# An encoder with two expert layers: the overflow blocks reordered, and identity products placed in the routing

## The reference, cut to what matters

```python
def expert_block(args):
    xb, e = args
    return (jax.nn.silu(xb @ w_gate[e]) * (xb @ w_up[e])) @ w_down[e]
yb = lax.map(expert_block, (xs, block_expert)).reshape(cap, D)
out = out.at[slot_tok].add(yb.astype(jnp.float32) * slot_w[:, None])
```

## Time and profile before

| what | value |
|---|---|
| median of 3 runs | 1425.97 us (1424.84 to 1427.04) |
| profiled execution, its own time | 1427.76 us |
| its span | 1426.0 us |
| TensorE busy | 1287.0 us (90%) |
| VectorE busy | 969.6 us (68%) |
| ScalarE busy | 618.0 us (43%) |
| share of the chain that ended last | PE 77%, DVE 12%, ACT 4%, DMA 4% |
| mean DMA rate | 251 GB/s over the span |

### The profile page before, as it was taken

The page is one execution under the profiler, slowest core; times in us unless marked ns, Lnnn a source line. Parts: engine busy times, 40 slices in busy tenths (PEclk is TensorE's granted clock), DMA queues, the critical chain, the costliest instruction groups (busy, mean ns, idle before and its releaser), DMA issues.

```text
span 1426.0 us, 14722 instructions
## 1 busy us (share of the span) xinstructions
PE 1287.0 (90%) x5057; PEld 864.6 (61%) x5057; DVE 969.6 (68%) x1379; ACT 618.0 (43%) x795; POOL 160.6 (11%) x169
## 2 busy tenths in 40 slices
PE   2999899949999999987999999998499999999886
PEld 2566665536666667743788854467367666667432
DVE  8678875576777777726766587856667777776153
ACT  3486401235555555504222167734355555554002
POOL 6000000010000000011000057710100000000200
PEclk9999899969999999999899999999599999999999
DMA  9636674258999999894365230024589999998641
GB/s 352 227 111 244 221 278 164 94 200 300 370 365 366 368 377 376 308 362 150 103 252 177 89 118 1 1 74 159 220 317 372 376 369 364 372 376 304 232 188 59
DMA packets 78114, 347.81 MB, mean 244 GB/s; under 512 B 12500, under 2 KB 12684, under 8 KB 69104
## 3 DMA queue, kind: packets, MB, share of 16 engines
q1 hardware_dynamic: 67184, 325.70, 61.4%
q0 software_dynamic: 7344, 16.68, 3.3%
q10 hardware_dynamic: 3536, 4.79, 0.9%
HBM read 334.15 MB, written 23.07 MB: 251 GB/s over the span
## 4 chain that ended last, share of the span: by engine, by line
PE 77%; DVE 12%; ACT 4%; DMA 4%; issue 2%; POOL 0%; SPq 0%; DVEq 0%; ACTq 0%; POOLq 0%
PE ps L1911 24%; PE ps L1922 16%; PE ps L2023 9%; PE ps L1831 4%; PE ps L1902 3%; PE ps L1793 3%; PE ps L1838 2%; PE ps L1897 2%; PE ps L1798 2%; DVE scratch L1027 2%; PE ps L2067 2%; PE ps L2095 2%; PE ps L2081 2%; DMA x_res<-in_x_dram 1%; DVE slab_ring_r L1449 1%
## 5 line engine op out<-in xcount | busy, mean ns | idle before, releaser
L1922 PE MATMUL ps<-slab_ring,scratch 128*128 128x512 f32 x560 | 246.5, 593 | 3.4 <-ACT scratch L935 2.1
L1911 PE MATMUL ps<-slab_ring_r,gate_rows_r 128*128 128x512 f32 x512 | 202.1, 395 | 0.0
L1922 PEld LDWEIGHTS ps<-slab_ring,scratch 128*128 128x128 f32 x560 | 105.8, 190 | 124.2 <-issue 117.2
L1449 DVE TENSOR_TENSOR slab_ring_r<-slab_ring,h_t_r 128x2048 fp32r<-128x2048 f32 x64 | 143.9, 2288 | 16.8 <-ACT h_t_r L852 16.8
L2023 PE MATMUL ps<-slab_ring_r 128*128 128x512 f32 x384 | 123.1, 402 | 4.1 <-DVE h_t_r L1084 4.1
L852 ACT ACTIVATE h_t_r<-slab_ring 128x2048 fp32r<-128x2048 f32 x64 | 118.6, 1901 | 0.0
L1911 PE MATMUL ps<-h_t_r,gate_rows_r 128*128 128x512 f32 x256 | 105.7, 413 | 12.5 <-issue 7.6
L881 ACT ACTIVATE scratch<-ps,mod_ab 128x128 f32<-128x128 f32 x128 | 48.1, 456 | 143.8 <-PE ps L1897 143.8
L1911 PEld LDWEIGHTS ps<-slab_ring_r,gate_rows_r 128*128 128x128 f32 x512 | 97.9, 191 | 19.2 <-issue 0.5
L1911 PE MATMUL ps<-h_t_r,scratch_r 128*128 128x512 f32 x256 | 102.9, 402 | 0.0
L1449 DVE TENSOR_TENSOR slab_ring_r<-slab_ring,mod_ring_r 128x2048 fp32r<-128x2048 f32 x32 | 73.3, 2292 | 41.0 <-ACT mod_ring_r L852 41.0
(11 more groups left out here) (343 smaller groups left out, 2303.0 us busy)
## 6 DMA issues: line engine op xcount, KB each, us to landing
slab_ring<-in_expert_w_gate_dram SPq DMA_DIRECT2D x35, 2048.0 KB, 9.5
slab_ring<-in_expert_w_up_dram SPq DMA_DIRECT2D x35, 2048.0 KB, 9.9
slab_ring<-in_expert_w_down_dram SPq DMA_DIRECT2D x35, 2048.0 KB, 9.7
mod_ring<-in_mod_w_dram SPq DMA_DIRECT2D x40, 512.0 KB, 4.5
y_rows<-scratch SPq DMA_DIRECT2D x32, 512.0 KB, 10.3
slab_ring<-in_mod_w_dram SPq DMA_DIRECT2D x32, 512.0 KB, 4.8
slab_ring<-in_mod_w_dram SPq DMA_DIRECT2D x12, 1024.0 KB, 11.5
slab_ring<-in_w_qkv_dram SPq DMA_DIRECT2D x6, 2048.0 KB, 12.0
```

The costliest lines, as they stand in the source:

```text
L1449: tt_(rest, w, top.bitcast(F32), ALU.subtract).then_inc(low_ready[c], 1)
L1911: ins = pe.matmul(ps[:, bank, :], x, w, start=(kt == 0 and i == 0), stop=(kt == KT - 1 and i == 2))
L1922: ins = pe.matmul(ps[:, 5 + h, :], hidT[:, f, :], w[:, 2 * f + h, :], start=(f == 0), stop=(f == FT - 1))
```

## The change

It has these parts.

- **Turning inside the last step.** The rows of overflow block 0 are turned inside the last expert's step, before its up product, and scaled there by ScalarE and VectorE (`xst_over(0)`). Rows of block k+1 are turned after the down product of block k, ahead of its mixing. The wait for `yb_ready` now stands behind the gate and up products. TensorE reads `n_over` in step 1.
- **Sums moved on VectorE.** `over_mask` is parted from the scaling, `combine(0)` now stands ahead of `over_hid(0)`.
- **Table load moved.** ScalarE ends `experts` with a root of a spare column, so that the table for Sqrt is loaded there.
- **SP.** The store of the last expert's output in layer 0 is issued before the load of the second `w_qkv` slab, not before the third.
- **POOL.** The gather of overflow block 0 is unconditional.
- **Loops.** On TensorE each turn of the overflow loop has three Ifs in place of one, on ScalarE two.
- **Identity products.** `keep_clock(n)` puts n fp32 products of the 128x128 identity with itself into PSUM bank 3: 6 ahead of the last `turn_x`, 3 ahead of the last `logits`, 26 ahead of the rank sums, 17 ahead of the second slot sum and 14 ahead of step 0, in each layer. Nothing reads them.

```diff
 SP, layer 0
                 for w, used in enumerate((gate_done, up_done, down_done)):
+                    if w == 1:
+                        store(NE - 1, 1)
                     sp.wait_ge(used, e0 + NE)
-                    if w == 2:
-                        store(NE - 1, 1)
                     load_slab(("qkv", w), w_qkv[:, :, w * HALF:(w + 1) * HALF])
...
 ScalarE
+            act.wait_ge(up_done, e0 + NE - 1)
+            xst_over(0)
             take_hid(NE - 1)
...
                 with act.If(k < n_over):
-                    act.wait_ge(o["turned"], k + 1)
-                    for kt in range(4):
...
+                with act.If(k + 1 < n_over):
+                    xst_over(k + 1)
+            act.activation(spare[:, l:l + 1], eps[:, 0:1], ACT.Sqrt)
...
 VectorE
+                if last:
+                    v.wait_ge(up_done, e + e0)
+                    xst_over(0)
                 v.wait_ge(silu_done, e + (e0 + 1))
...
             with v.If(n_over > 0):
-                over_in(0)
+                over_mask(0)
+            combine(0)
+            with v.If(n_over > 0):
                 over_hid(0)
-            for t in range(TT):
+            for t in range(1, TT):
                 combine(t)
...
                     with v.If(k < n_over):
+                        xst_over(k)
                         over_y(k)
                         for t in range(TT):
                             over_add(k, t)
-                        over_in(k)
+                        over_mask(k)
                         over_hid(k)
...
 TensorE
+            def keep_clock(products):
+                for _ in range(products):
+                    pe.matmul(ps[:, 3, 0:P], ident[:, :], ident[:, :], start=True, stop=True)
...
+            keep_clock(6)
             turn_x(s, TT - 1)
+            keep_clock(3)
             logits(TT - 1)
+            keep_clock(26)
             pe.wait_ge(hot_ready, TT * (l + 1))
...
             ins.then_inc(slots_summed, 1)
+            keep_clock(17)
...
+                if last:
+                    pe.wait_ge(o["xs"], 16)
+                    turn_xs(0, o["turned"])
                 pe.wait_ge(low_ready[1], 2 * e + (2 * e0 + 2))
...
             turn_xs(0, xs_turned)
+            keep_clock(14)
             step(0, 0, 0, first=1)
...
-            pe.wait_ge(yb_ready, e0 + NE)
...
                 with pe.If(k < n_over):
-                    pe.wait_ge(o["xs"], (k + 1) * 16)
-                    pe.wait_ge(o["added"], k * TT + 1)
-                    turn_xs(0, o["turned"])
+                    pe.wait_ge(o["added"], k * TT + 2)
                     pe.wait_ge(o["xst"], (k + 1) * 2)
...
                     product(over_slab[1], 3, o["gu"])
+                    pe.wait_ge(yb_ready, e0 + NE)
...
                     down(over_slab[2], o["down"])
+                with pe.If(k + 1 < n_over):
+                    pe.wait_ge(o["xs"], k * 16 + 32)
+                    turn_xs(0, o["turned"])
+                    pe.wait_ge(o["xst"], k * 2 + 4)
+                    pe.sem_inc(turn_seen, 1)
+                with pe.If(k < n_over):
                     pe.wait_ge(o["yb"], k + 1)
```

More of the change, by code:

```diff
@@ L192, in build @@
     eps = small("eps", [P, 1])
+    spare = small("spare", [P, LAYERS])
     modc = small("mod_cols", [P, KT])
@@ L697, in gather_over @@
                                       bounds_check=S - 1, oob_is_err=False).then_inc(o["xs"], 16)
-            with gp.If(n_over > 0):
-                gather_over(0)
+            gather_over(0)
             for par in range(2):
@@ L916, in experts, with xst_over @@
                     step(2 * i + par, par, i)
+            o = over[l]
+            def xst_over(k):
+                act.wait_ge(o["turned"], k + 1)
+                for kt in range(4):
+                    ins = act.activation(xsT[0][:, kt, :], ps[:, 0, kt * P:(kt + 1) * P], ACT.Identity, bias=AB[:, s, 1, kt:kt + 1], scale=AB[:, s, 0, kt:kt + 1])
+                ins.then_inc(o["xst"], 1)
             step(NE - 2, 0, NE // 2 - 1)
             step(NE - 1, 1, NE // 2 - 1, last=True)
+            act.wait_ge(up_done, e0 + NE - 1)
+            xst_over(0)
             take_hid(NE - 1)
-            o = over[l]
-            act.wait_ge(route_ready, l + 1)
             n_over = act.value_load(info[0:1, 7:8], min_val=0, max_val=MAX_OVER)
@@ L925, in experts @@
                 with act.If(k < n_over):
-                    act.wait_ge(o["turned"], k + 1)
-                    for kt in range(4):
-                        ins = act.activation(xsT[0][:, kt, :], ps[:, 0, kt * P:(kt + 1) * P], ACT.Identity, bias=AB[:, s, 1, kt:kt + 1], scale=AB[:, s, 0, kt:kt + 1])
-                    ins.then_inc(o["xst"], 1)
                     act.wait_ge(o["gate"], k + 1)
@@ L1520, in experts, with xst_over @@
                 step(2 * i + 1, 1, i)
+            o = over[l]
+            def xst_over(k):
+                v.wait_ge(o["turned"], k + 1)
+                for kt in range(4, KT):
+                    ins = ts(xsT[0][:, kt, :], ps[:, 1, (kt - 4) * P:(kt - 3) * P], AB[:, s, 0, kt:kt + 1], AB[:, s, 1, kt:kt + 1], ALU.mult, ALU.add)
+                ins.then_inc(o["xst"], 1)
             step(NE - 2, 0, NE // 2 - 2)
+            v.sem_inc(o["added"], TT)
             step(NE - 1, 1, NE // 2 - 1, last=True)
             take_y(NE - 1, 1, NE // 2 - 1)
-            o = over[l]
             n_over = v.value_load(info[0:1, 7:8], min_val=0, max_val=MAX_OVER)
@@ L1533, in experts, with over_mask @@
             link(tt_(early_w, early_w, both_w, ALU.mult))
[L1534 to L1541, removed]
+            def over_mask(k):
                 ts(match, yplace[:, 0, :], block_no, None, ALU.is_equal).then_inc(o["mask"], 1)
@@ L1940, in step @@
                 pe.wait_ge(xst_dve, e + (e0 + 1))
+                if first == 2:
+                    pe.wait_ge(route_ready, l + 1)
+                    n_over = pe.value_load(info[0:1, 7:8], min_val=0, max_val=MAX_OVER)
                 if first != 1:
@@ L1956, in step @@
                     turn_xs(1 - par, xs_turned)
+                if last:
+                    pe.wait_ge(o["xs"], 16)
+                    turn_xs(0, o["turned"])
                 pe.wait_ge(low_ready[1], 2 * e + (2 * e0 + 2))
                 split_product(par, 1, 3, range(KT)).then_inc(up_done, 1)
+                if first == 2:
+                    return n_over
+            o = over[l]
             pe.wait_ge(xs_filled[0], (NE // 2) * l * 16 + 16)
             turn_xs(0, xs_turned)
+            keep_clock(14)
             step(0, 0, 0, first=1)
-            step(1, 1, 0, first=2)
+            n_over = step(1, 1, 0, first=2)
             with pe.Fori(1, NE // 2 - 1) as i:
@@ L1970, in experts @@
             down_product(NE - 1, 1, NE // 2 - 1)
-            o = over[l]
             over_slab = [slab(("exp", l, c, 0)) for c in range(3)]
-            pe.wait_ge(yb_ready, e0 + NE)
-            pe.wait_ge(route_ready, l + 1)
-            n_over = pe.value_load(info[0:1, 7:8], min_val=0, max_val=MAX_OVER)
             pe.sem_inc(o["mixed"], TT)
```

## The result

The changed kernel takes 1412.76 us (median of 4 runs, 1411.52 to 1414.12) against 1425.9 for the kernel before beside it: ratio 0.9902, 95% interval 0.989 to 0.9915. The forecast was 1401.0 (1393 to 1409). The sign was right, but only about half of the 25 us came. The profiled execution took 1413.72 us, its span is 1412.0 (before 1427.76 and 1426.0).

A forecast was written before the change was run, and what follows sets the result against it. The kernel was taken as TensorE-bound (77% of the chain), with gains only where TensorE waits or its clock falls. 3.3 + 1.7 + 10.3 + 9.7 = 25.0 us off the median 1425.97 gave 1401.0, range 1393 to 1409.

The forecast's parts named there:

- Part 1: Routing: identity products keep TensorE's clock up, half gates fall to 2.77 us; 3.3 us in layer 0, 1.7 in layer 1.
- clock not held: Rival in the routing: identity products don't hold the clock and cost 0.45 us each; 1417 us, chance 0.06.
- loads not overlapped: Rival in the routing: weight loads don't pass beside products at full clock, a product takes 0.43 us; 1414, chance 0.04.
- slower: Rival in the routing: loads don't overlap and the clock is lower, 0.87 us a product; 1477 us, chance 0.02.
- Part 2: Layer 0's overflow: rows turned in step 15, products follow at once, scaling starts 9.0 us earlier; 10.3 us (2 to 12.5).
- Each lands after 5.4 to 5.7: Layer 0's overflow: the first two y gathers land by 639.3, so hidden rows start at 642.1, 0.7 us late.
- second `w_qkv` slab: Layer 0's overflow: loaded 11 us later but wanted only some 40 us later, so it costs nothing.
- The 8.4 us from mixing to turn: Layer 0's overflow: six empty loop turns on TensorE's sequencer, 1.4 us each, put the next turn 8.4 after mixing begins.
- Part 3: Layer 1's overflow: first block gains, second block's gate product starts earlier, table load saves 1.2; 9.7 us (7 to 13).
- The first block gains as in layer 0: Layer 1's overflow: products end at 1351.4 instead of 1358.8, the down product 7.1 us earlier at 1361.2.
- forecast wait of 1.9 us for the second block's rows: Layer 1's overflow: these rows land at about 1363, after the down product ends at 1361.2, so TensorE waits 1.9 us.
- the hidden rows wait for the gathers: Rival in the overflow: gathers take 7.7 and 9.5 us, layer 0 keeps 2, layer 1 about 5; 1414, chance 0.08.

The follow-up runs named there:

- e4: The kernel before with the 6, 3, 26, 17 and 14 identity products alone: 1422.5 us, ratio 0.9968.
- e9: The changed kernel with the two w_qkv slabs held until the last y rows have landed, in layer 0 only: 1407.5 us, ratio 0.9864.
- e2: The changed kernel with w_qkv slabs (layer 0) and the second overflow block's weights (layer 1) held until the last y rows landed: 1397.9 us, ratio 0.9807.
- e5: e2 with TensorE's second overflow-loop branch nested inside the first, so an empty turn has one branch instead of three: 1397.9 us, ratio 0.9802.
- e1: The changed kernel with the first overflow block's hidden rows ahead of combine(0) on VectorE, as before the change: 1418.9 us, ratio 0.9949.
- e3: The changed kernel with both edits, loads held as in e2 and hidden rows ahead of combine(0) as in e1: 1403.1 us, ratio 0.9833.
- e6: e5 with the second block's rows gathered ahead of the y rows, turned behind the first block's up product and scaled behind the hidden rows: 1397.5 us.
- e10: The changed kernel with only the second overflow block's weights in layer 1 held until the last y rows have landed: 1403.5 us, ratio 0.9836.
- e11: e6 with, in layer 1, the first block's output scaled ahead of VectorE's last pair of adds: 1398.0 us, ratio 0.9792.
- e8: e2 with ten more identity products ahead of step 1's gate product in each layer, into an idle PSUM bank: 1397.5 us, ratio 0.9795.

## Why the prediction was right or wrong

**Part 1 was right.** An identity product costs 0.23 us at 2.4 GHz (0.22 taken). The products hid, but for the last 14 (4.92 against 3.1 us), and the half gates went to 2.78 us in layer 0 and 3.01 in layer 1 by the chain. I had expected one fall of the clock ahead of the 17 and full clock behind; they ran at full clock (34 records in 4.04 us), and the fall came within the 14. Layer 0 gave 2.15 + 0.8 = 3.0 of 3.3 us, layer 1 1.8 of 1.7; e4 confirms it alone. The rivals "clock not held", "loads not overlapped" and "slower" are out. The rule of the Trainium skill ("TensorE: Matmul & The Clock Gate", The mechanism) that a weight load overlaps a running matmul only when the row group differs would have made a product 0.43 (the prediction's estimate, twice its 0.22); the trace, with 0.23, doesn't agree.

**Part 2 failed in one step**: "Each lands after 5.4 to 5.7". I took that landing from a stretch in which one slab had been under way for 8 us, and put two whole slabs behind the store without asking what they do to the gathers behind it. They landed after 11.5 to 12.0 us. The same oversight stands in the term of the second `w_qkv` slab, "loaded 11 us later": I put it at nothing, because I looked only at who wants the slab and not at what it meets. e9, which holds the slabs back, gives 5.3 us. No run tests SP's old order alone. The store itself was timed well (3.2 against 2.6). From this follow the hidden rows forecast 0.7 late (TensorE waited 4.86 us for them) and, what counted, the other six adds forecast to end at 650.7: they waited for gathers three times more (1.56 us the longest) and ended at 654.63. From the last down product's start to the scaling it was 40.93 us before; I forecast 31.1, the changed kernel has 36.74 and e2 30.53. So 3.4 of the 9.0 came, and all of it with the loads held. The rest of layer 0 was mis-sized the other way: from the scaling on I counted 1.3 and measured 3.6 (332.23 to 328.67); 2.8 of them lie in the QKV stage, of which less ran at the lower clock (from its first product to attention's first 148.91 us before, 146.12 after). I had no term for this, so this part of the gain is luck. The 8.4 us from mixing to turn were right: 8.55, and e5 shows why.

**Part 3 failed in the same way, and worse.** "The first block gains as in layer 0" overlooked that the earlier gate product calls up the next block's weights among the gathers. Of 9.7 us 3.95 - 0.8 = 3.1 came. With that load held it was 12.8. The forecast wait of 1.9 us for the second block's rows did not appear, because all else was later; e1 shows what they cost once it is not.

**The rival** "the hidden rows wait for the gathers", given 0.08 and 1414, hit the time and the place. Its price in layer 0 (2 us kept) was off by 5, in layer 1 (5 kept) by 2, and e1 shows that in layer 0 the hidden rows' wait is a symptom: the adds that wait for the last gather bind. My argument against it, that the slab is behind the store now, was the mistake: behind the store is in front of the gathers. With the loads held both layers together gave 13.1 + 12.8 = 25.9 us, more than the 20.0 I had summed. The change's idea was worth more than I forecast, and the transfers left 10.1 us of it.

## What to carry to other kernels

When an edit makes a product earlier, list every load that waits for that product, and see which small transfers it will now meet: here two waits that hold back weights not wanted for ten us and more were worth 15 us, more than the 13 of the whole change. Time every transfer of a group and not the first alone; the chain of waits names the one that binds, here the last of eight in layer 0 and the second in layer 1. Do the same for a load whose place in a queue the edit moves. And give an engine the work that needs nothing yet while it would otherwise idle: with the two adds ahead of the hidden rows the kernel is 5 us faster (e2 against e3).

## What the runs showed of the hardware

- A y gather of 512 KB (one of eight, issued 1.3 us apart) lands in 5.4 to 6.4 us where the loads are held (medians of e2, e3, e6, e9, e10), in 9.6 to 12.3 beside two w_qkv slabs of 2 MB (layer 0 of the changed kernel, e1 and e10), and in 15.2 to 16.9 beside the gate and up weights, 2 MB each (layer 1 of the changed kernel, e1 and e9). The gather of the second block's rows, also 512 KB, took 3.7 us in e2, 14.3 in the changed kernel, and 19.5 in e1, where a further 2 MB load met it.
- TensorE's clock fell behind single waits of 3.59, 4.86, 7.15 and 12.41 us, in e6 behind 2.23, and in e11 behind 1.00 and 0.69, but not behind the 2.66 ahead of layer 1's mixing in e2 and in the changed kernel. Behind the wait of 2.46 us in step 1 it fell in 14 of 22 cases (two layers, eleven profiles). So the length of the last wait alone does not tell. The products of 7.13 us behind a fall took 8.6 to 10.1.
- Kernels that do the same work up to layer 0's last turn reached it between 284.51 and 287.30 us in their profiled executions. Stretches of full and lower clock lie differently in each. A difference of 2 us between the totals of single executions is therefore none. Stretches between anchors tell more: the last one lies between 82.46 and 82.82 us in e2, e5, e8 and e10. But a stretch can hold one fall more or less, some 1.6 us each.
